# Modulation's rows turned into columns in groups, and the value means of retention scaled on ScalarE

## What is computed

```python
mod = c_act @ w_ada + b_ada                       # 6 * 1024 numbers for each layer
shift1, scale1, gate1, shift2, scale2, gate2 = jnp.split(mod, 6, axis=-1)
h = modulate(rms_norm(x, norm1_g), shift1, scale1)
...
ret = retention(heads(rq, RET_DK), heads(rk, RET_DK), heads(rv, RET_DV))
ret = head_group_norm(ret, ret_norm_g)            # takes off the mean over a head's 128 columns
...
x = x + gate1 * mixed
h2 = modulate(rms_norm(x, norm2_g), shift2, scale2)
...
x = x + gate2 * y
```

## Time and profile before

| what | value |
|---|---|
| timed runs | 2967.64, 2970.6, 2971.73 us; median 2970.6 us |
| the profiled execution, its own time | 2969.3 us |
| its span, first to last instruction | 2967.5 us |
| what lies around the span | 1.8 us |
| TensorE matmul busy | 2913.7 us, 98% of the span |
| VectorE, ScalarE, GpSimd busy | 36%, 36%, 40% |
| mean granted TensorE clock | 0.994 of 2.4 GHz |

### The profile page before, as it was taken

One profiled execution on the slowest core, in us unless ns is written; L12 is line 12 of the kernel. 1 busy time (PEld: TensorE's weight loads), 2 busy tenths in 40 slices (PEclk: granted clock), 3 DMA queues, 4 the chain that ended last, 5 costly groups with the idle time before them and its releaser, 6 DMA issues.

```text
span 2967.5 us, 36647 instructions
## 1 busy us (share of the span) xinstructions
PE 2913.7 (98%) x15555; PEld 2436.5 (82%) x15555; DVE 1071.9 (36%) x1856; ACT 1078.8 (36%) x1640; POOL 1175.3 (40%) x502
## 2 busy tenths in 40 slices
PE   6999999999999999999999999999999999999999
PEld 4888888888888878888898888988888877888887
DVE  3533473266564634322242220441110266521102
ACT  3324433343322424432243332343222366432221
POOL 1432245434445432344444444435444333244442
PEclk8999999999999999999999999999999999999999
DMA  7332254345554422233333333324333322233332
GB/s 232 102 111 57 79 185 128 86 142 194 190 193 141 114 64 59 78 93 96 89 100 99 94 94 98 93 79 114 93 98 97 90 72 67 76 93 100 93 97 73
DMA packets 529686, 315.09 MB, mean 106 GB/s; under 512 B 16210, under 2 KB 507380, under 8 KB 529268
## 3 DMA queue, kind: packets, MB, share of 16 engines
q1 hardware_dynamic: 529524, 312.75, 35.9%
HBM read 310.61 MB, written 2.10 MB: 105 GB/s over the span
## 4 chain that ended last, share of the span: by engine, by line
PE 94%; DVE 3%; ACT 2%; issue 0%; DMA 0%; POOL 0%; SPq 0%; DVEq 0%; ACTq 0%
PE b L419 22%; PE b L421 21%; PE b L420 21%; PE o L419 5%; PE o L421 5%; PE o L420 5%; PE b L462 1%; PE b L463 1%; PE b L464 1%; PE o L821 1%; PE s L704 1%; PE s L801 1%; PE b L1002 1%; PE b L1004 1%; PE b L1003 0%; ACT aT L1414 0%
## 5 line engine op out<-in xcount | busy, mean ns | idle before, releaser
L2726 POOL TENSOR_TENSOR lo<-raw,hi 128x1024 fp32r<-128x1024 f32 (+1 forms) x492 | 1173.1, 2392 | 1754.5 <-ACT hi L1265 1754.1
L419 PE MATMUL b<-HH,hi 128*128 128x512 f32 x1792 | 714.1, 398 | 6.0 <-ACT rv L1431 2.6
L421 PE MATMUL b<-HH,lo 128*128 128x512 f32 x1792 | 699.4, 390 | 0.0
L420 PE MATMUL b<-HL,hi 128*128 128x512 f32 x1792 | 699.1, 390 | 0.0
L1265 ACT ACTIVATE hi<-raw 128x1024 fp32r<-128x1024 f32 (+1 forms) x492 | 507.6, 1039 | 412.4 <-DMA raw<-in_w_down_dram 105.2
L419 PEld LDWEIGHTS b<-HH,hi 128*128 128x128 f32 x1792 | 337.2, 188 | 86.0 <-issue 14.6
L421 PEld LDWEIGHTS b<-HH,lo 128*128 128x128 f32 x1792 | 337.1, 188 | 71.6
L420 PEld LDWEIGHTS b<-HL,hi 128*128 128x128 f32 x1792 | 337.3, 188 | 70.9 <-issue 1.9
L419 PE MATMUL b<-FH,hi 128*128 128x512 f32 (+1 forms) x594 | 218.1, 367 | 0.0
L420 PE MATMUL b<-FL,hi 128*128 128x512 f32 (+1 forms) x594 | 217.1, 365 | 0.0
L421 PE MATMUL b<-FH,lo 128*128 128x512 f32 (+1 forms) x594 | 217.1, 365 | 0.0
(11 more groups left out here) (484 smaller groups left out, 4423.8 us busy)
## 6 DMA issues: line engine op xcount, KB each, us to landing
raw<-in_w_up_dram SPq DMA_DIRECT2D x88, 512.0 KB, 3.9
raw<-in_w_in_dram SPq DMA_DIRECT2D x80, 512.0 KB, 4.3
raw<-in_w_ada_dram SPq DMA_DIRECT2D x80, 512.0 KB, 4.9
raw<-in_w_mg_dram SPq DMA_DIRECT2D x48, 512.0 KB, 3.8
raw<-in_ffn_w_gate_dram SPq DMA_DIRECT2D x44, 512.0 KB, 3.8
raw<-in_ffn_w_up_dram SPq DMA_DIRECT2D x44, 512.0 KB, 3.8
raw<-in_w_down_dram SPq DMA_DIRECT2D x32, 512.0 KB, 4.0
raw<-in_ffn_w_down_dram SPq DMA_DIRECT2D x32, 512.0 KB, 3.9
```

The costliest lines, as they stand in the source:

```text
L419: e.matmul(out, wh, xh, start=start and k == 0, stop=False)
L420: e.matmul(out, wh, xl, start=False, stop=False)
L421: mm = e.matmul(out, wl, xh, start=False, stop=stop and k == last)
L2726: e.tensor_tensor(t["lo"][:, s, 0:w], K.raw[:, s, 0:w], t["hi"][:, s, 0:w].bitcast(F32), ALU.subtract).then_inc(*m.lo.up(n))
```

## The change

Modulation's rows are folded in groups: rows 4 to 6, 7 to 9 and 10 to 11 of layer 0, and rows 0 to 3, 4 to 7 and 8 to 11 of layer 1. Each row's sums go to their own 16 columns of `AS`, now 64 wide, and after a group's last row the four matmuls run once with 8 to 16 columns, and one addition writes the group's part of `MOD`. Only the first row of a group waits for the fold before it. The other part: VectorE no longer scales the sums of the retention's values; ScalarE does that itself with one ACTIVATE of 128 x 4, waits for it, and then copies the values out.

```diff
+ADA_LAST = ((6, 9, 11), (3, 7, 11))
+
+def ada_group(l, q_):
+    first = 0 if l else 4
+    for last in ADA_LAST[l]:
+        if q_ <= last:
+            return range(first, last + 1)
+        first = last + 1
...
 def ada(self, l, q_):                 # the same in TensorSteps and in VectorSteps
...
-        self.unfolded = (l, q_)
+        if q_ in ADA_LAST[l]:
+            self.unfolded = (l, q_)
...
 def ada_fold(self, l, q_):            # TensorE
         b = self.take_bank(("col", l, q_))
+        n = len(ada_group(l, q_))
         q.wait_ge(m.vnorm.at("ada", l, q_, "s"), self.free[b])
         for c in range(4):
-            mm = e.matmul(self.bank[b][32 * c:32 * c + 32, 0:4], t["fold"], t["AS"][:, c:16:4], start=True, stop=True)
+            mm = e.matmul(self.bank[b][32 * c:32 * c + 32, 0:4 * n], t["fold"], t["AS"][:, c:16 * n:4], start=True, stop=True)
...
 def take(u):                          # ScalarE, ret_values
-            q.wait_ge(m.vtake.at("rvm", l, c, u))
+            N = t["RVM"][:, 8 * c + 4 * u:8 * c + 4 * u + 4]
+            q.wait_ge(m.vtake.at("rvs", l, c, u))
+            e.activation(N, N, ACT.Copy, scale=-1.0 / 128).then_inc(*m.atake.up(("rvm", l, c, u)))
+            q.wait_ge(m.atake.at("rvm", l, c, u))
...
 def ada_add(self, l, q_):             # VectorE
-        c = pcol(l, "b_ada")
+        rows = ada_group(l, q_)
+        c, a, z = pcol(l, "b_ada"), 4 * rows[0], 4 * q_ + 4
         q.wait_ge(m.stat.at("col", l, q_), m.vnorm.at("par", 3))
-        e.tensor_tensor(t["MOD"][:, l, 4 * q_:4 * q_ + 4], self.out_of(("col", l, q_))[:, 0:4],
-                        t["PAR"][:, c + 4 * q_:c + 4 * q_ + 4], ALU.add).then_inc(*m.vnorm.up(("mod", l, q_)))
+        e.tensor_tensor(t["MOD"][:, l, a:z], self.out_of(("col", l, q_))[:, 0:z - a], t["PAR"][:, c + a:c + z],
+                        ALU.add).then_inc(*m.vnorm.up(*[("mod", l, r) for r in rows]))
...
 def ada_sums(self, l, q_, n, room):   # VectorE
-        q.wait_ge(m.vnorm.at("ada", l, q_, "t"), m.stat.at("col", *((l, q_ - 1) if q_ else (l - 1, 11))))
-        e.tensor_reduce(t["AS"][:, :], room.rearrange("p (b i) -> p b i", i=32), AXX, ALU.add).then_inc(
+        i = ada_group(l, q_).index(q_)
+        q.wait_ge(m.vnorm.at("ada", l, q_, "t"),
+                  m.stat.at("col", *((l, q_ - 1) if q_ else (l - 1, 11))) if i == 0 else None)
+        e.tensor_reduce(t["AS"][:, 16 * i:16 * i + 16], room.rearrange("p (b i) -> p b i", i=32), AXX, ALU.add).then_inc(
...
 def take(u):                          # VectorE, ret_values
-            q.wait_ge(m.vtake.at("rvs", l, c, u))
-            e.tensor_scalar(N, N, -1.0 / 128, None, ALU.mult).then_inc(*m.vtake.up(("rvm", l, c, u)))
...
-        fixed("AS", [128, 16])
+        fixed("AS", [128, 64])
```

## The result

The changed kernel takes 2975.0 us (median of 21 runs, 2972.4 to 2976.9). The kernel before took 2969.6 us beside it (21 runs, 2967.6 to 2972.6). The ratio is 1.0018 with a 95% interval of 1.0011 to 1.0024: slower by 5.4 us, where 2958.0 was forecast, outside the range of 2952 to 2965. The profiled execution took 2974.45 us, with a span of 2972.7 and a mean granted clock of 0.993.

A forecast was written before the change was run, and what follows sets the result against it. TensorE, its matmuls busy 98% of the span, was taken as the bound. 4.8 + 0.96 + 4.38 + 0.36 + 1.62 - 0.1 = 12.0 us gave 2957.3 or 2958.6, forecast 2958.0 us, eight-in-ten range 2952 to 2965.

The forecast's parts named there:

- The folds taken out: On TensorE, thirteen removed plain folds at 0.37 us each were to save 4.8 us.
- The first fold: Where only b0 and b1 rotate, removing this fold and the wait for VectorE's copy behind it was to gain 0.96 us.
- Layer 1's first tiles: Three more matmuls were to fit in before the wait for VectorE's update at layer 1's start, gaining 0.36 us.
- The tile `small`: In layer 1, a bank read out earlier was to remove a 2.56 us wait and 1.8 us of low clock: 4.38 us.
- The attention's first tiles: In the last attention, the new bank order was to remove TensorE's wait at the first tiles, gaining 1.62 us.
- rival (a): Waits move to other late data rather than go, only the folds' own 5.2 us stay: 2965.4 us; chance 0.10.
- Kept folds: The six remaining folds, widened from 4 to at most 16 columns, were to cost 0.1 us, 0.25 at most.
- Rival (c): Matmuls of 16 strided columns cost as much as four of 4; only the banks' gain stays: 2963.6 us; chance 0.04.
- Rival (b): Low clock stretches behind remaining waits appear or go, giving 2960 or 2956 us; chance 0.20 for both together.
- New low stretches of the clock: A sign listed as showing the prediction wrong, if they appeared in TensorE's granted clock; no size given.
- The scale on ScalarE: Scaling value means there was to be hidden: 0, bounds -0.1 and +0.2 us; about 1.1 us if `small`'s collision stayed.
- (d): Slower: VectorE's attention operations fall more often under GpSimd's subtractions, 2.1 us a hit, 3.9 with low clock; chance 0.03.

## Why the prediction was wrong

**The folds taken out: right.** In the run with the areas moved back, the matmuls behind the 13 plain folds stand 5.1 us earlier than before, against 4.8 in the sum; the removed fold's spacing is the forecast one. The 0.3 come from the steps behind a fold, beyond the spacing that was read: four or five of them are some ns longer, 0.02 us a fold, so that a fold costs 0.40 us and not 0.37.

**The first fold: right**, 0.96 us (0.95 in the changed kernel) against 0.96. **Layer 1's first tiles: right**, 0.36. **The tile `small`: right**, 4.4 us against 4.38, wait and low clock both gone. **The attention's first tiles: right**, 1.7 against 1.62. The five together make 12.4 us in the trace, and rival (a), that these waits would move, is refuted: TensorE's list of waits of the changed kernel has nothing new in these stages. **Kept folds: right**, 0.1 us. Their records last 195 ns at the median, before 183, and in the trace with the areas moved back the spacing at a kept fold is 835 ns with 8 columns, 841 with 12 and 849 with 16, where it was 828 with 4; the six together cost 0.10 us. So the widening is not free, and the floor under the starts of small matmuls that the prediction cites is not seen here: a fold's eight records start 6 to 7 ns apart, with one step of 32 to 34. Rival (c) falls with the 0.46 us spacing (12.0 less 5.2 in the prediction's own terms gives 2963.8 for it, not 2963.6).

**Rival (b), the clock: in part.** Low stretches do come and go between the traces. With the areas moved back, the trace has none at layer 1's start and none near 2546 us, but one in the attention that lasts longer than before; by the starts of the matmuls this gives back 1.5 us and takes 1.3. The trace of the groups alone lacks the one in the attention. "New low stretches of the clock" were a sign of being wrong, and the changed kernel has one, at layer 1's start, for 1.6 us; it is not what turned the result.

**The scale on ScalarE: right in this change**, 0 by the pair of runs with and without it beside the groups, and 2.2 us alone. The prediction gave 1.1 us for the case that the collision stayed; what it left out of that figure is that a wait of 1.43 us is not followed by a low clock at this place where one of 2.56 was.

**The sum itself held**: the changed kernel with the areas where they belong is 14.1 us faster than before (10.1 to 17.5 by the interval), against 12.0 in the sum. In the two traces the last product matmul stands 13.5 us earlier, and 1.1 of that is there at the first product matmul already (31.30 against 32.43), ahead of anything that differs; 12.4 us lie between.

**The step that failed** is one that the prediction doesn't have. "Kept folds get wider" costs the wider fold as an instruction, and nothing costs the wider tile. The line `fixed("AS", [128, 64])` was in the diff, it moves every area behind it by 128 bytes, and some 4050 of TensorE's product matmuls stream from there. No edit had more instructions under it, and it was taken for nothing without a word. What it cost: 18.0 us alone, 19.7 (2975.0 less 2955.3, two sets of runs) in the changed kernel, where the traces show 18.0 between the first and the last product matmul. Against the 12 to 14 us of gain this is the whole difference in sign. The trace of before holds no product matmul at another distance, so the size couldn't have been read from it; but as a change whose price no row shows, it ought to have been named and given a range on both sides. The rival for "slower", (d), was about hits on VectorE in the attention, and had nothing to do with it.

## What to carry to other kernels

When a diff resizes a tile, work out where the tiles behind it go, and treat each operand whose start changes as changed. When the result doesn't fit, compare the mean duration of untouched lines form by form before looking for waits: 389 to 395 ns on a line that the change doesn't touch led to the answer here. Read steps of a few ns from unrounded starts: a timeline rounded to 10 ns moved the means of single steps in these traces by over 3 ns. And where a change does two things, as with groups of folds and the rotation of banks, count the rotation through: here it was worth more than the work saved.

## What the runs showed of the hardware that I had not expected

The pace of 512-column matmuls depends on how far the moving operand starts from the weights modulo 256 bytes: 226.7 ns a step at 0 (and at 256, where the changed kernel's areas were moved back to), 229 at 64, 233.3 at 32, 128 and 192 (fp32r data, 128 x 128 weights loaded for each matmul beside the stream). 256 columns go from 120.2 ns at 0 to 115.3 at 192. Moving both operands together by 128 bytes makes no difference: the ratio is 0.9999.

The best kernel of these runs is the changed one with `big` at 128 more than a multiple of 256: 2955.3 us, faster than the kernel before by 0.47% (0.34 to 0.59%) and than the kernel after by 0.66% (2955.3 against 2975.0).
